# Moving the squares behind the casts at the entry of the first up projection

## The chip, the cores and the metric

One core of a Trainium2 chip runs the whole computation in one launch. The metric is the device time of that launch in microseconds. The engines that matter here are TensorE (PE, matmuls), VectorE (DVE), ScalarE (ACT), GpSimd (POOL), and SyncE (SP), which only issues the loads.

## The reference, cut to what matters

The reference is two blocks of two layers each over 512 positions of width 1024. The change touches the first layer's pool mixer and the entry of the first conv FFN:

```python
x = x + pool_mixer(rmsnorm(x, norm_mix[0]), pool_w[0], pool_scale[0])
x = x + conv_ffn(rmsnorm(x, norm_ffn[0]), ffn_up[0], ffn_conv[0], ffn_conv_b[0], ffn_down[0])
...
def conv_ffn(h, w_up, conv_w, conv_b, w_down):
    u = h @ w_up                                  # 1024 -> 2 * 2816
    up = jnp.pad(u, ((0, 0), (CONV_W - 1, 0), (0, 0)))
    u = sum(conv_w[j] * up[:, j:j + S] for j in range(CONV_W)) + conv_b
    a, g = u[..., :D_FF], u[..., D_FF:]
    return (jax.nn.silu(g) * a) @ w_down
```

## The kernel before, in words

Activations lie transposed: `x` is eight chunks of 128 rows (features) by 512 columns (positions). Each fp32 matmul operand is split into a rounded high part and the low part that is left, and a product of 128 by 128 by 512 is three matmuls (`three`, L510 to L512): high by high, high by low, low by high. One output bank of the up projection takes eight chunks, so 24 matmuls. This text calls that a product. Products come in pairs: for each `f` of 22, `g = 0` is the a-half and `g = 1` the gate half. The first pair is the first and second product, the next pair the third and fourth. PE runs them in order, `u = f % 2`, into banks `2u` and `2u + 1`.

Weights come in jobs of 1 MB, one job for each pair of products, double-buffered in two slots. SP loads a job into `w_raw` once the low part of the job two before it is done (`load`). ACT copies it to `w_hi` (`split_w`, L1109), once PE has finished the pair that used the slot. DVE subtracts to get `w_lo` (`split_w`, L1684). Job 0 is the pool mixer's, job 1 the first pair's, job 2 the second pair's, job 3 the third pair's. The change calls job 1, 2, 3 the first, second and third split of this stage in that sense.

Each engine has its own instruction queue, written out by hand, and works it off in order. Between the queues stand semaphores. At the entry the work of one chunk `m` of `x` goes like this.

- PE: `mix(m)` of the pool mixer ends.
- DVE: `residual(m)` adds it to `x` (L1701, with a wait for its own write behind it).
- ACT: `hi_of_x` casts `x` times gain to `h_hi` (L1136); DVE: `split_x` makes `h_lo` from `x` and `h_hi` (L1696). PE's first product takes chunk `k` as soon as `h_lo` has it.
- ACT: `square` writes `x` squared to the one buffer `sq` (L1139); POOL: `add` adds it to `sq_sum` (L2517). `square(m)` waits until the add of `m - 1` has freed `sq`.

The normalisation is applied behind the matmul: PE sums `sq_sum` over partitions with a matmul by ones (`stats`, L523), ACT takes the root (`root`), DVE the reciprocal (`norm_factors`, L1690), and then DVE multiplies each finished bank by `rs` into `taps_in` (L1777), which frees the bank. PE meets a full ring at the fifth product, which needs the bank of the first.

ACT's queue has in this order: all casts and squares of the pool stage, then in `conv_up(0)` the second split, `root`, and the loop over `f`. DVE's has: the residuals and low parts, the second split, `norm_factors`, and the loop. In both loops the split for the pair two ahead stands in the body of `f`. `pairs` makes a hardware loop over two `f` at a time and takes the last two (with `peel=1` also the first two) out of it, so that they can differ.

`taps_in` has three columns of zero padding, so it is cleared once; the clearing also gives the four credits of `acc_free` that PE starts with.

Of the kernel before, what the change touches and what calls it, by code (L numbers as in the profile page):

```python
# [27 lines left out]
ALU = mybir.AluOpType  # L28
ACT = mybir.ActivationFunctionType
# [6 lines left out]
ND = D // P  # L36
DFF = 2816
NF = DFF // P
# [157 lines left out]
def build(nc, a, stop_after=None):  # L196
    with ExitStack() as ctx:
# [194 lines left out]
            return (g_hi[:, k], g_lo[:, k]) if n == 2 and k < EARLY else (h_hi[:, k], h_lo[:, k])  # L392

        partner_of = (sq_sum, sq)
        query_of = [qr[c % 3][:] for c in range(ND - 1)] + [taps_in[:, 0, PAD:]]
        y_of = [hid[:, 0], hid[:, 1], sq[:], silu_g[:], taps_in[:, 0, PAD:], taps_in[:, 1, PAD:], hid[:, 0], hid[:, 1]]
        squares_of = (hid[:, 0], hid[:, 1], sq[:], silu_g[:])
# [109 lines left out]
        def _(pe):  # L507
# [43 lines left out]
            def up(n):  # L551
                stage = f"up{n}"

                def body(i):
                    for u in range(2):
                        f, slot = 2 * i + u, (J0[stage] + u) % 2
                        pe.wait_ge(w_lo_done, J0[stage] + f + 1)
                        for g in range(2):
                            pe.wait_ge(acc_free, FREE0[stage] + 2 * f + g - 3)
                            for k in range(ND):  # L560
                                if u == 0 and g == 0:
                                    pe.wait_ge(h_lo_done, H_COUNT[stage] + k + 1)
                                mm = three(bank[2 * u + g][:], *tile_of(slot, g * ND + k), *input_of(n, k),
                                           k == 0, k == ND - 1)
                            mm.then_inc(seg_done, 1)
                            if isinstance(i, int) and 2 * f + g == (1 if n == 0 else 0):
                                (stats_of_both if n == 2 else stats)(stage)
                pairs(pe, NF // 2, body, peel=1)

# [528 lines left out]
        def _(act):  # L1098
            def split_w(j, count=None, segs=None):


                if j >= n_jobs:
                    return
                act.wait_ge(w_loaded[j % 2], 16 * (j // 2 + 1) if count is None else count)
                if j >= 2:

                    act.wait_ge(seg_done, SEGS_BEFORE[j - 1] if segs is None else segs)
                n = TILES[j] * P
                act.activation(w_hi[j % 2][:, 0:n], w_raw[j % 2][:, 0:n], ACT.Copy).then_inc(w_hi_done, 1)  # L1109
# [45 lines left out]
            def conv_up(l):  # L1155
                stage = f"up{l}"
                n0, j0, s0 = l * NF, J0[stage], SEG0[stage]

                split_w(j0 + 1)
                root(stage)  # L1160

                def body(i):
                    for u in range(2):
                        f, j = 2 * i + u, j0 + u + 2

                        if not isinstance(i, int):
                            split_w(j, 16 * (j // 2 + 1) + 16 * i, s0 + 2 * f + 2)
                        elif f < NF - 1:
                            split_w(j0 + f + 2)

                        act.wait_ge(hid_done, n0 + f)
                        for g in (1, 0):
                            wait_apart(acc_free, FREE0[stage] + 2 * f + 2)
                            act.activation(bank[CONV_A + g][:], taps_in[:, g, PAD:], ACT.Identity,  # L1174
                                           bias=col(f"conv{l}_b", g * NF + f), scale=col(f"conv{l}_2", g * NF + f))\
                                .then_inc(seeded, 1)
                        act.wait_ge(tapped, 4 * (n0 + f) + 3)
                        act.activation(silu_g[:], bank[CONV_G][:], ACT.Silu).then_inc(silu_done, 1)
                        wait_apart(hid_done, n0 + f + 1)
                        act.activation(act_hi[:, f], hid[:, u], ACT.Copy).then_inc(act_hi_done, 1)  # L1180
                pairs(act, NF // 2, body)

            def glu_up(n):
                stage = f"up{n}"
# [106 lines left out]
            def pool():  # L1291

                def average_hi(m):
                    act.wait_ge(pool_u_done, m + 1)
                    act.activation(h_hi[:, m], bank[4 + m % 4][:], ACT.Copy, scale=col("mix0", m)).then_inc(pool_hi_done, 1)

                def residual_hi(m):

                    act.wait_ge(seg_done, m // 2 * 2 + 2)
                    act.wait_ge(x_ready, x_before("up0") + m + 1)  # L1300
                    hi_of_x("up0", m)

                act.wait_ge(vec_loaded, 16)
                average_hi(0)
                average_hi(1)
                act.activation(w_hi[0][:, HALF_POOL:], w_raw[0][:, HALF_POOL:], ACT.Copy).then_inc(w_hi_done, 1)
                for m in range(2, 6):
                    average_hi(m)
                split_w(1)
                average_hi(6)  # L1310
                average_hi(7)
                for m in range(ND):
                    residual_hi(m)
                    if m >= 2:
                        act.wait_ge(sq_added, 9 * PREP_OF["up0"] + m - 1)
                        square("up0", m - 2)
                for m in (ND - 2, ND - 1):
                    act.wait_ge(sq_added, 9 * PREP_OF["up0"] + m + 1)
                    square("up0", m)

            def attention_inputs():
                split_w(J0["kproj"] + 1)
# [354 lines left out]
        def _(dve):  # L1677
# [48 lines left out]
            def pool():  # L1726
# [17 lines left out]
                                  ALU.subtract).then_inc(w_lo_done, 1)  # L1744
                average_lo(2)
                average_lo(3)
                dve.memset(taps_in[:], 0.0).then_inc(acc_free, 4)
                for m in range(2):
                    residual(m)
                average_lo(4)  # L1750
                average_lo(5)
                split_w(1)
                for m in (2, 3):
                    residual(m)
                average_lo(6)
                average_lo(7)
                split_x("up0", 0)
# [7 lines left out]
            def conv_up(l):  # L1765
                stage = f"up{l}"
                n0, j0, s0 = l * NF, J0[stage], SEG0[stage]

                split_w(j0 + 1)
                norm_factors(stage)  # L1770

                def body(i):
                    for u in range(2):
                        f = 2 * i + u
                        for g in range(2):
                            dve.wait_ge(seg_done, s0 + 2 * f + g + 1)
                            dve.tensor_tensor(taps_in[:, g, PAD:], bank[2 * u + g][:], rs[:], ALU.mult).then_inc(acc_free, 1)  # L1777
                        if not isinstance(i, int) or f < NF - 1:
                            split_w(j0 + u + 2 if not isinstance(i, int) else j0 + f + 2, j0 + f + 3)
                        for n, (tap, g) in enumerate(((1, 1), (1, 0), (0, 1), (0, 0))):  # L1780
                            if tap == 1:
# [9 lines left out]
                        dve.wait_ge(act_lo_done, n0 + f)  # L1791
                        dve.tensor_tensor(hid[:, u], bank[CONV_A][:], silu_g[:], ALU.mult).then_inc(hid_done, 1)
                        dve.wait_ge(hid_done, n0 + f + 1)
                pairs(dve, NF // 2, body)

            def glu_up(n):
                stage = f"up{n}"
# [708 lines left out]
        def _(pool):  # L2506
# [5 lines left out]

            def add(prep, m):
                n = PREP_OF[prep]
                pool.wait_ge(sq_done, ND * n + m + 1)
                pool.wait_ge(sq_added, 9 * n + m + 1)
                pool.tensor_tensor(sq_sum[:], sq_sum[:], sq[:], ALU.add).then_inc(sq_added, 1)  # L2517

            def squares(prep):
                clear(prep)  # L2520
# [154 lines left out]
                        .then_inc(y_lo, 1)  # L2675

            pool.memset(pool_tap[:], 0.0).then_inc(act_lo_done, 1)
            for stage in enabled:
                if stage.startswith("up"):
                    split_hidden(int(stage[2:]))  # L2680
# [192 lines left out]
```

## Time and profile before

| what | value |
|---|---|
| time, median of 3 runs | 3060.1 us (3057.92 to 3061.3) |
| time of the profiled execution | 3060.17 us |
| its span, first to last instruction | 3058.4 us |
| PE busy | 2989.5 us, 98% of the span |
| DVE, ACT, POOL busy | 1594.9, 1194.0, 528.3 us |
| mean granted TensorE clock | 0.991 |

The profiled execution's time is 1.8 us more than its span, and 0.07 us above the median. The span begins with the first instruction of any engine; all times in the rows below count from there. A busy PE is not PE at its peak, since matmuls are pipelined: a 512-column matmul lasts 0.39 us in the rows but the next starts 0.23 us behind it.

### The profile page before, as it was taken

Reading aid. Unit: us, or ns where it says so; the run is one execution under the profiler, and the core shown is the slowest. Engines: PE = TensorE matmul, PEld = TensorE weight load, DVE = VectorE, ACT = ScalarE, POOL = GpSimd, SP = SyncE. Lnnn points to the kernel's source line nnn. Section 1 sums busy time; section 2 is a strip of 40 time slices with the busy share of each in tenths; the row PEclk is TensorE's granted clock in tenths of the full one; section 3 lists DMA queues with packets and bytes.
Section 4 is the critical chain, followed back from the end, with each engine's and each line's share of the span. In section 5 each row is a group of like instructions: output and inputs, shape, how many; then the busy total and the mean of one; then the engine's idle time right before and its main releaser. Section 6 shows DMA issues by size and latency. Waiting matters only on the chain.

```text
span 3058.4 us, 37147 instructions
## 1 busy us (share of the span) xinstructions
PE 2989.5 (98%) x13546; PEld 2455.6 (80%) x13546; DVE 1594.9 (52%) x1838; ACT 1194.0 (39%) x1589; POOL 528.3 (17%) x516
## 2 busy tenths in 40 slices
PE   7999999999999999999999899999999999999998
PEld 6888877777888888788887688888888887788887
DVE  6665366687566535533338843333433337743332
ACT  5554243488455424322232442222322226532221
POOL 1111011255211112111110211111111104511110
PEclk9999999999999999999999999999999999999999
DMA  4222333200222223222232022222322232222222
GB/s 165 96 96 84 101 119 102 76 1 1 86 97 98 83 94 113 96 96 92 85 112 85 15 83 96 96 89 95 106 96 96 82 110 97 83 97 96 92 86 84
DMA packets 47931, 273.42 MB, mean 89 GB/s; under 512 B 6448, under 2 KB 8160, under 8 KB 25568
## 3 DMA queue, kind: packets, MB, share of 16 engines
q1 hardware_dynamic: 47840, 272.19, 25.7%
q8 instruction: 58, 0.95, 0.1%
q14 instruction: 33, 0.27, 0.0%
HBM read 269.28 MB, written 2.11 MB: 89 GB/s over the span
## 4 chain that ended last, share of the span: by engine, by line
PE 89%; DVE 6%; ACT 2%; issue 1%; POOL 1%; DMA 0%; DVEq 0%; ACTq 0%; SPq 0%; POOLq 0%
PE bank L510 28%; PE bank L512 28%; PE bank L511 28%; PE bank L822 1%; DVE w_lo L1684 1%; ACT probs L1394 1%; PE bank L960 1%; PE bank L728 0%; PE bank L806 0%; DVE rc L2395 0%; PE bank L839 0%; PE bank L838 0%; PE bank L926 0%; PE bank L807 0%; POOL r_lo L2674 0%
## 5 line engine op out<-in xcount | busy, mean ns | idle before, releaser
L510 PE MATMUL bank<-h_hi,w_hi 128*128 128x512 f32 x2448 | 961.7, 393 | 12.9 <-DVE w_lo L1684 7.8
L511 PE MATMUL bank<-h_lo,w_hi 128*128 128x512 f32 x2448 | 955.6, 390 | 0.0
L512 PE MATMUL bank<-h_hi,w_lo 128*128 128x512 f32 x2448 | 955.5, 390 | 0.0
L1684 DVE TENSOR_TENSOR w_lo<-w_raw,w_hi 128x2048 fp32r<-128x2048 f32 (+2 forms) x282 | 575.3, 2041 | 527.8 <-ACT w_hi L1109 527.1
L1109 ACT ACTIVATE w_hi<-w_raw 128x2048 fp32r<-128x2048 f32 (+2 forms) x282 | 474.9, 1684 | 328.3 <-PE bank L512 301.1
L510 PEld LDWEIGHTS bank<-h_hi,w_hi 128*128 128x128 f32 x2448 | 460.3, 188 | 117.0 <-DVE w_lo L1684 11.3
L512 PEld LDWEIGHTS bank<-h_hi,w_lo 128*128 128x128 f32 x2448 | 460.5, 188 | 97.3
L511 PEld LDWEIGHTS bank<-h_lo,w_hi 128*128 128x128 f32 x2448 | 460.5, 188 | 96.4 <-issue 1.9
L510 PE MATMUL bank<-act_hi,w_hi 128*128 128x512 f32 x1056 | 411.6, 390 | 4.4 <-DVE w_lo L1684 4.4
L511 PE MATMUL bank<-act_lo,w_hi 128*128 128x512 f32 x1056 | 411.3, 390 | 0.0
L512 PE MATMUL bank<-act_hi,w_lo 128*128 128x512 f32 x1056 | 411.3, 389 | 0.0
L2542 POOL TENSOR_TENSOR act_lo<-hid,act_hi 128x512 f32 (+1 forms) x132 | 171.8, 1301 | 1274.5 <-ACT act_hi L1202 847.3
L2517 POOL TENSOR_TENSOR sq_sum<-sq_sum,sq 128x512 f32<-128x512 f32 x87 | 123.5, 1420 | 824.3 <-ACT sq L1139 824.3
L510 PEld LDWEIGHTS bank<-act_hi,w_hi 128*128 128x128 f32 x1056 | 198.3, 188 | 46.3 <-DVE w_lo L1684 5.6
L1813 DVE TENSOR_TENSOR hid<-bank,rs 128x512 f32<-128x512 f32 x88 | 60.9, 692 | 331.6 <-PE bank L512 331.6
L512 PEld LDWEIGHTS bank<-act_hi,w_lo 128*128 128x128 f32 x1056 | 198.3, 188 | 41.3
L511 PEld LDWEIGHTS bank<-act_lo,w_hi 128*128 128x128 f32 x1056 | 198.3, 188 | 41.1
L1202 ACT ACTIVATE act_hi<-hid 128x512 f32 (+1 forms) x88 | 55.8, 634 | 410.8 <-DVE hid L1816 410.8
L1136 ACT ACTIVATE h_hi<-x,vec 128x512 fp32r<-128x512 f32 (+1 forms) x72 | 51.9, 723 | 366.2 <-DVE x L1701 366.2
L1701 DVE SCALAR_TENSOR_TENSOR x<-bank,x 128x512 f32 (+1 forms) x72 | 49.7, 691 | 254.1 <-PE bank L512 254.1
L1200 ACT ACTIVATE silu_g<-taps_in 128x512 f32<-128x512 f32 x88 | 55.7, 633 | 264.3 <-DVE taps_in L1810 264.3
L1786 DVE SCALAR_TENSOR_TENSOR bank<-taps_in,vec,bank 128x512 f32<-128x512 f32 x176 | 120.0, 750 | 1.8 <-ACT bank L1174 1.8
(373 smaller groups left out, 3207.3 us busy)
## 6 DMA issues: line engine op xcount, KB each, us to landing
w_raw<-in_w_up SPq DMA_DIRECT2D x132, 1024.0 KB, 4.9
w_raw<-in_w_down SPq DMA_DIRECT2D x96, 704.0 KB, 4.0
w_raw<-in_w_wout SPq DMA_DIRECT2D x12, 1024.0 KB, 4.9
w_raw<-in_w_ple SPq DMA_DIRECT2D x16, 640.0 KB, 3.9
w_raw<-in_w_ein SPq DMA_DIRECT2D x6, 1024.0 KB, 4.9
w_raw<-in_w_kproj SPq DMA_DIRECT2D x4, 1024.0 KB, 5.1
w_raw<-in_w_qproj SPq DMA_DIRECT2D x4, 1024.0 KB, 4.9
w_raw<-in_w_ogate SPq DMA_DIRECT2D x4, 1024.0 KB, 4.9
```

Source lines behind the costliest of these rows:

```text
L510: pe.matmul(out, wh, mh, start=first, stop=False)
L511: pe.matmul(out, wh, ml, start=False, stop=False)
L512: return pe.matmul(out, wl, mh, start=False, stop=final)
L1109: act.activation(w_hi[j % 2][:, 0:n], w_raw[j % 2][:, 0:n], ACT.Copy).then_inc(w_hi_done, 1)
L1136: act.activation(h_hi[:, m], x[:, m], ACT.Copy, scale=col(GAIN[prep], m)).then_inc(h_hi_done, 1)
L1200: act.activation(silu_g[:], taps_in[:, u, PAD:], ACT.Silu).then_inc(silu_done, 1)
L1202: act.activation(act_hi[:, f], hid[:, u], ACT.Copy).then_inc(act_hi_done, 1)
L1684: dve.tensor_tensor(w_lo[j % 2][:, 0:n], w_raw[j % 2][:, 0:n], w_hi[j % 2][:, 0:n].bitcast(F32), ALU.subtract).then_inc(w_lo_done, 1)
L1786: dve.scalar_tensor_tensor(out=acc, in0=taps_in[:, g, PAD - back:PAD - back + T], scalar=col(f"conv{l}_{tap}", g * NF + f), in1=acc, op0=A ...
L1813: dve.tensor_tensor(hid[:, u], bank[2 * u + 1][:], rs[:], ALU.mult).then_inc(acc_free, 1)
L2517: pool.tensor_tensor(sq_sum[:], sq_sum[:], sq[:], ALU.add).then_inc(sq_added, 1)
L2542: pool.tensor_tensor(act_lo[:, f], hid[:, u], act_hi[:, f].bitcast(F32), ALU.subtract)\
```

## The change

The square buffers become two, `sq` and `silu_g`. ACT's queue holds all eight casts first and all eight squares behind them; a square waits only for the add two before it. POOL starts its adds when all eight low parts are done. PE's `stats` moves from behind the second product to behind the third. ACT and DVE issue the third split right behind the second and ahead of `root` and `norm_factors`, and for that the first two `f` are taken out of their loops. DVE's third residual moves ahead of the first split, and the clearing of `taps_in` moves from DVE to the head of POOL's queue. Only the first up projection (`l == 0`, `n == 0`) is meant; other stages keep their order.

```diff
+        first_squares = (sq[:], silu_g[:])
...
-                            if isinstance(i, int) and 2 * f + g == (1 if n == 0 else 0):
+                            if isinstance(i, int) and i == 0 and 2 * f + g == {0: 2}.get(n, 0):
                                 (stats_of_both if n == 2 else stats)(stage)
...
                 split_w(j0 + 1)
+                if l == 0:
+                    split_w(j0 + 2)
                 root(stage)
...
-                        if not isinstance(i, int):
+                        if l == 0 and isinstance(f, int) and f == 0:
+                            pass
+                        elif not isinstance(i, int):
                             split_w(j, 16 * (j // 2 + 1) + 16 * i, s0 + 2 * f + 2)
                         elif f < NF - 1:
                             split_w(j0 + f + 2)
...
-                pairs(act, NF // 2, body)
+                pairs(act, NF // 2, body, peel=1 - l)
...
                 for m in range(ND):
                     residual_hi(m)
+                for m in range(ND):
                     if m >= 2:
-                        act.wait_ge(sq_added, 9 * PREP_OF["up0"] + m - 1)
-                        square("up0", m - 2)
-                for m in (ND - 2, ND - 1):
-                    act.wait_ge(sq_added, 9 * PREP_OF["up0"] + m + 1)
-                    square("up0", m)
+                        act.wait_ge(sq_added, 9 * PREP_OF["up0"] + m)
+                    act.activation(first_squares[m % 2], x[:, m], ACT.Square).then_inc(sq_done, 1)
...
-                dve.memset(taps_in[:], 0.0).then_inc(acc_free, 4)
                 for m in range(2):
                     residual(m)
                 average_lo(4)
                 average_lo(5)
+                residual(2)
                 split_w(1)
-                for m in (2, 3):
-                    residual(m)
+                residual(3)
                 average_lo(6)
                 average_lo(7)
...
                 split_w(j0 + 1)
+                if l == 0:
+                    split_w(j0 + 2)
                 norm_factors(stage)
...
-                        if not isinstance(i, int) or f < NF - 1:
+                        if not isinstance(i, int) or f < NF - 1 and (l or f):
                             split_w(j0 + u + 2 if not isinstance(i, int) else j0 + f + 2, j0 + f + 3)
...
-                pairs(dve, NF // 2, body)
+                pairs(dve, NF // 2, body, peel=1 - l)
...
             def add(prep, m):
                 n = PREP_OF[prep]
+                if n == 0:
+                    pool.wait_ge(h_lo_done, ND)
                 pool.wait_ge(sq_done, ND * n + m + 1)
                 pool.wait_ge(sq_added, 9 * n + m + 1)
-                pool.tensor_tensor(sq_sum[:], sq_sum[:], sq[:], ALU.add).then_inc(sq_added, 1)
+                square = sq[:] if n else first_squares[m % 2]
+                pool.tensor_tensor(sq_sum[:], sq_sum[:], square, ALU.add).then_inc(sq_added, 1)
...
             pool.memset(pool_tap[:], 0.0).then_inc(act_lo_done, 1)
+            pool.memset(taps_in[:], 0.0).then_inc(acc_free, 4)
```

## Rows read from the trace of the kernel before

**Rows 1.** The page: span, and engines of the chain that ended last.

```profile
span 3058.4 us, 37147 instructions
...
PE 89%; DVE 6%; ACT 2%; issue 1%; POOL 1%; DMA 0%; DVEq 0%; ACTq 0%; SPq 0%; POOLq 0%
```

**Rows 2.** Timeline of PE: start, duration, instruction, [idle before, releaser].

```profile
34.17 0.50 PE L510 MATMUL bank<-h_hi,w_hi 128*128 128x512 f32 x1 [0.59 <-DVE x L1701]
...
37.55 0.50 PE L510 MATMUL bank<-h_hi,w_hi 128*128 128x512 f32 x1 [1.04 <-DVE h_lo L1696]
...
41.58 0.79 PE L510 MATMUL bank<-h_hi,w_hi 128*128 128x512 f32 x1 [1.03 <-DVE h_lo L1696]
...
45.23 0.39 PE L510 MATMUL bank<-h_hi,w_hi 128*128 128x512 f32 x1
...
50.71 1.02 PE L523 MATMUL bank<-sq_sum,ones 128*128 128x512 f32 x2
...
51.80 0.40 PE L511 MATMUL bank<-h_lo,w_hi 128*128 128x512 f32 x1
...
62.47 0.39 PE L510 MATMUL bank<-h_hi,w_hi 128*128 128x512 f32 x1
...
2584.06 0.58 PE L510 MATMUL bank<-h_hi,w_hi 128*128 128x512 f32 x1 [3.86 <-DVE w_lo L1684]
```

**Rows 3.** Windows: stretch, length, busy of five engines (instructions), clock, DMA, GB/s.

```profile
42.00:43.00 1.00, 1.00 (x3) 0.74 (x3) 1.00 (x2) 0.00 (x0) 1.00 (x1) 0.50 0.00 0
...
2586.00:2587.00 1.00, 1.00 (x4) 0.71 (x4) 1.00 (x1) 0.99 (x3) 0.76 (x2) 0.50 1.01 418
```

**Rows 4.** Timeline of DVE around the entry.

```profile
20.35 0.92 DVE L1747 MEMSET taps_in<- 128x1030 f32 x1 [0.16 <-issue]
...
28.11 1.53 DVE L1701 SCALAR_TENSOR_TENSOR x<-bank,vec,x 128x512 f32<-128x512 f32 x2
29.68 1.41 DVE L1730 SCALAR_TENSOR_TENSOR h_lo<-bank,vec,h_hi 128x512 fp32r<-128x512 f32 x2
...
35.39 0.74 DVE L1701 SCALAR_TENSOR_TENSOR x<-bank,vec,x 128x512 f32<-128x512 f32 x1
36.17 1.33 DVE L1696 SCALAR_TENSOR_TENSOR h_lo<-x,vec,h_hi 128x512 fp32r<-128x512 f32 x1
...
40.21 3.67 DVE L1696 SCALAR_TENSOR_TENSOR h_lo<-x,vec,h_hi 128x512 fp32r<-128x512 f32 x3
47.85 2.29 DVE L1684 TENSOR_TENSOR w_lo<-w_raw,w_hi 128x2048 fp32r<-128x2048 f32 x1 [3.98 <-ACT w_hi L1109]
...
56.08 1.29 DVE L1777 TENSOR_TENSOR taps_in<-bank,rs 128x512 f32<-128x512 f32 x2 [0.24 <-DVE rs L1690]
```

**Rows 5.** Source views of L1696 and L1684: durations in ns, minimum, median, maximum.

```profile
L1696 DVE SCALAR_TENSOR_TENSOR h_lo<-x,vec,h_hi x72: 737/752/1782, 31.0 to 2686.4; 128x512 fp32r<-128x512 f32 x42, - x30
...
L1684 DVE TENSOR_TENSOR w_lo<-w_raw,w_hi x282: 557/2291/3354, 25.9 to 3032.6; 128x2048 fp32r<-128x2048 f32 x84, 128x1408 fp32r<-128x1408 f32 x48, 128x1280 fp32r<-128x1280 f32 x8, 128x384 fp32r<-128x384 f32 x1
```

**Rows 6.** Timeline of POOL, at the entry and at two later places.

```profile
31.20 1.70 POOL L2517 TENSOR_TENSOR sq_sum<-sq_sum,sq 128x512 f32<-128x512 f32 x1 [29.90 <-ACT sq L1139]
...
44.06 1.28 POOL L2517 TENSOR_TENSOR sq_sum<-sq_sum,sq 128x512 f32<-128x512 f32 x1 [0.74 <-ACT sq L1139]
...
609.04 1.26 POOL L2578 TENSOR_TENSOR oq<-qr,oq 64x512 fp32r<-64x512 f32 x1 [0.17 <-POOL oq L2578]
...
1194.07 1.32 POOL L2532 TENSOR_TENSOR sq_sum<-sq_sum,sq 128x512 f32<-128x512 f32 x1 [1.91 <-ACT sq L1224]
1195.36 1.74 POOL L2535 TENSOR_TENSOR hid<-hid,silu_g 128x512 f32<-128x512 f32 x1
```

**Rows 7.** Timeline of ACT around the entry.

```profile
43.36 0.63 ACT L1139 ACTIVATE sq<-x 128x512 f32<-128x512 f32 x1 [1.72 <-POOL sq_sum L2517]
45.38 0.63 ACT L1139 ACTIVATE sq<-x 128x512 f32<-128x512 f32 x1 [1.39 <-POOL sq_sum L2517]
45.91 1.91 ACT L1109 ACTIVATE w_hi<-w_raw 128x2048 fp32r<-128x2048 f32 x1
```

## The prediction

> **What bounds the kernel now.** I read the page first. The chain that ended last lies on PE for 89% of the span of 3058.4 us [rows 1], and the profiled execution took 3060.17 us, 0.07 above the median of the runs, so the sum below can be added to that median. What delays PE at the entry is carried to the end unless something behind it waits on another engine. Second comes PE's timeline from the first to the fifth product. PE should do a matmul each 0.227 us (47 of them lie between 51.80 and 62.47) [rows 2]. The first product starts at 34.17 and the second only at 45.23, 11.06 us later, where 24 matmuls need 5.45. The reader sees two causes: three waits of about 1.04 us for low parts (two stand in the rows), and a slow stretch behind the last of them. From 41.58 to 45.23 lie 9 matmuls that would take 2.04 us and took 3.65, so it cost 1.6, and the granted clock there is 0.50, the 1.2 GHz level [rows 2, 3]. Third comes DVE: the three waits follow its rhythm of residual and low part. A low part takes 1.33 us there and 1.22 in the group of three [rows 4], but over all 72 of its kind the minimum is 0.737 and the median 0.752 [rows 5]. The slow ones lie where POOL adds squares (44.06, among others, beside the group of three that runs to 43.88) [rows 4, 6]. Fourth come ACT and POOL: the last square starts at 45.38, 0.04 us behind the end of an add (44.06 + 1.28), and the cast of the second split only 0.53 behind that, at 45.91 [rows 6, 7]. Its low part runs from 47.85 to 50.14 [rows 4]. PE reaches the statistics at 50.71 and needs the second split right after [rows 2]. So before, two chains end almost together: low parts and first two products at 50.71, second split at 50.14.
>
> **The DVE chain.** With the adds held back, a low part costs its median 0.75, or 0.67 from start to start (two of nearly the same kind take 1.41 together) [rows 4, 5]. A residual costs 0.78 to the next start, with its wait (35.39 to 36.17) [rows 4]. The first split ends where it did, since it waits for its cast, and one of the two residuals at 28.11 now stands ahead of it. So the first low part starts at 28.11 + 0.78 + 2 x 0.67 = 30.23. Behind it stand 8 low parts and 4 residuals: 8 x 0.67 + 4 x 0.78 + 0.08 = 8.56, and the last ends at 38.79 instead of 40.21 + 3.67 = 43.88, 5.1 us earlier. The casts, 0.7 apart or more, keep ahead.
>
> **The first two products.** PE is through with the mixer at 33.58 (34.17 less the 0.59 idle before it) [rows 2], and by then its first bank and the first chunks are ready: the residual that frees the bank comes at 31.57. Chunk 5 waits for a low part that ends at 37.45, chunk 7 for the one at 38.79, so its three matmuls run to 39.57, and the second product to 39.57 + 5.48 (45.23 to 50.71) = 45.05. That is a gain of 5.66 us: the waits and the slow stretch are gone.
>
> **What is late next.** The second split. Its cast stands in ACT's queue behind all eight squares, and the eighth square waits for the sixth add. The adds now begin only at 38.79 + 0.07 = 38.86 (a square that ended at 43.99 released an add at 44.06) [rows 6, 7]. Each add also waits for the one before. The adds of before show no such back-to-back pair, since the square lay between. The nearest is the pair of POOL operations at 609.04 with 0.17 idle between them for their own semaphore; adds that follow each other without that wait start 1.29 apart [rows 6]. I take 1.28 + 0.17 = 1.45, the case with the wait, and keep 1.29 as the lower end. The upper end is 1.70, the one add at the entry that met two low parts of DVE [rows 6]. Step by step: sixth add ends at 38.86 + 5 x 1.45 + 1.28 = 47.39; square starts at 47.43; cast at 47.96, ends at 49.87; low part of the weights from 49.90, 2.29 us [rows 4, 7]. The eighth add runs until 50.29 beside it; for that I add 0.2. The second split is ready at about 52.4. A full overlap could make the low part 3.35, the maximum of its line [rows 5]: 1.1 more at the upper end.
>
> The price by rule instead of row: in the Trainium skill, GPSIMD Engine Reference, section Instruction dispatch, a two-input body needs about 2.5 cycles an element, which at that page's 1.2 GHz is an estimate of 1.07 us for 512. Six adds would then end about 1.3 us sooner, and the forecast would be about 2 us above before instead of 3.3. The adds here lasted 1.28 at best [rows 6], so the sum goes by the row.
>
> **The pause and the clock.** PE has nothing from 45.05 to 52.4: the statistics, which filled 50.71 to 51.5, are behind the third product now, and the third product is what waits. Queued behind it is all of PE. A pause of 3.86 us elsewhere left the clock at 0.50 still two to three us after the restart [rows 2, 3]. The slow stretch at the entry cost 1.6, and I charge that again; below it nothing (the clock keeps its 2.4 GHz level), above it a whole third product at the half rate, 5.45.
>
> **The statistics and the fifth product.** Third product 52.4 + 1.6 + 5.45 = 59.45, then statistics. All adds end by 50.29, so they don't wait. Before, from the statistics to the fifth product there were two products, 50.71 to 62.47 or 11.76; now there is one, 6.31. That gives 65.76 for the fifth product against 62.47: **3.3 us later**. The root, the reciprocal and the first `taps_in` keep their lag: 56.08 + 0.69 - 50.71 = 6.06 behind the statistics, so the first bank is free at 65.5, just in time (0.25 to spare, and that margin doesn't move with the pause). The third split comes right behind the second, done by about 54.7, ahead of its need at 65.8. The fourth split now follows the first `taps_in` and taps; DVE reaches it some 9 to 10 us behind the first `taps_in`, at about 75.5, and PE needs it at 65.76 + 10.9 = 76.6. That is the thinnest cover behind the entry, about 1 us; without it that much is paid.
>
> **Edits costed at nothing.** Clearing `taps_in` cost DVE 0.92, but there DVE next waits for the mixer's products and casts; on POOL it lies in 29.90 us of idleness before the first add [rows 4, 6]. The third split early, and the peeled loops, only move work of ACT and DVE under running products; the third split was in time before too, so having it earlier gains nothing. The first two squares run under the last low parts. SP's loads are released by the weights' low parts: job 4's by the second split, 2 us later than before, and it is used more than 15 us behind.
>
> **The sum.** -5.66 (second product's end), +7.35 (pause to 52.4), +1.6 (clock), and the statistics moved, not removed: 65.76 - 62.47 = +3.3 us. 3060.1 + 3.3 = **3063.4 us**. About 0.2%, 6.1 us, is what a measurement of this kernel can tell from no change.
>
> **Rivals.**
>
> - The wait does not appear. If the second split were ready by 45.05 as before it was ready ahead of PE, the whole 5.66 would stay: 3054.4. For it: the waits and the slow stretch that vanish are real. Against it: the cast stands behind the eighth square, and even at 1.29 for an add it can't be ready before 51.4. The sign turns where the second split is ready by about 49. Chance 0.04, and even then the gain is just below 0.2%.
> - The low parts don't get faster without the adds, because they are slow for another reason (both operands new, a pointer scalar). Then each takes 1.24 from start to start, the last ends 8 x 0.57 = 4.6 us later, and with it adds, second split and all behind: +7.9, 3068. Against it: the median of 0.752 in all other places [rows 5]. It decides, as slower by over 0.2%, from about 1.02 a low part on. Chance 0.05.
> - The slow clock lasts through the third product: 5.45 instead of 1.6, so +7.1, 3067.2. For it: the pause is twice any that I found before a product. Against it: 2.4 GHz came back within some 3.5 us in the stretches read. Chance 0.05.
> - Adds at 1.70 and a low part of 3.35: five starts at 0.25 more and a sixth duration of 0.42 more, and 1.1 less the 0.2 charged: +2.6 more, 3066. Inside the range.
>
> **How the numbers follow.** The likeliest, a pause of about 7 us with a price of 1.5 to 6, has 0.86. Its low end is 1.29 an add (-0.8) and no slow stretch (-1.6): 3061.0; its high end is 3066. The runs of before spread from 2.2 below to 1.2 above their median, so I take 3059.5 to 3067. Slower by over 0.2% holds the two rivals at 3067 to 3068 and the top of the likeliest case, 0.11; faster by over 0.2% is left 0.02 for what I don't see; within 0.2% has 0.87.
>
> **What would show it.** Right: low parts (L1696) of 0.75 at the entry, the last ending near 38.8; no half-rate matmuls in the first product; eight adds in a row from 38.9, about 1.45 apart; PE idle before the third product, released by `w_lo`, for about 7 us; half-rate matmuls behind it; the fifth product near 65.8. Wrong: low parts of over 1 us, an add pitch far from 1.45, a second split ready before 49, or a fifth product that waits for its bank or a seventh for the fourth split.

## The result, and the profile after

The changed kernel takes 3065.14 us (median of 20 runs, 3062.57 to 3065.89) against 3059.94 for the kernel before (20 runs, 3057.66 to 3061.6). That is 5.2 us more, a ratio of 1.0018 with an interval from 1.0012 to 1.0024. The forecast was 3063.4 in a range from 3059.5 to 3067. Two executions of well over 4000 us, one of `e7_third_late` (4603.08) and one of the kernel before in the same session (5987.33), are left out of the medians below.

The profiled execution has a span of 3062.0 us (its time is 3063.8). Its entry began 1.17 us earlier than in the profile before: the low part of the first split starts at 24.73 instead of 25.90 [rows 4]. So each time of before has 1.17 taken off when it is compared with this trace. First the page:

```profile
span 3062.0 us, 37083 instructions
...
PE 89%; DVE 7%; ACT 2%; issue 1%; POOL 1%; DMA 0%; DVEq 0%; ACTq 0%; SPq 0%; POOLq 0%
```

Its shares hardly differ from [rows 1]; 5 us in 3060 are not to be found there. The chain of the stretch from 34 to 70 us tells it (start, duration, what ended last):

```profile
35.50 2.09 DVE h_lo L1699 x3
37.66 1.30 POOL sq_sum L2524
39.12 1.30 POOL sq_sum L2524
...
44.95 1.27 POOL sq_sum L2524
46.35 0.43 issue
46.78 1.90 ACT w_hi L1110
48.71 2.54 DVE w_lo L1687
51.29 0.79 PE bank L511
```

Read it from the top. The last low part releases the first add, six adds follow one another, the sixth lets ACT do the eighth square and the cast of the second split, DVE makes its low part, and only then does PE's third product begin. PE's timeline:

```profile
36.31 0.50 PE L511 MATMUL bank<-h_hi,w_hi 128*128 128x512 f32 x1 [0.49 <-DVE h_lo L1699]
...
43.73 0.39 PE L513 MATMUL bank<-h_hi,w_lo 128*128 128x512 f32 x1
51.29 0.79 PE L511 MATMUL bank<-h_hi,w_hi 128*128 128x512 f32 x1 [7.17 <-DVE w_lo L1687]
...
56.15 0.63 PE L513 MATMUL bank<-h_hi,w_lo 128*128 128x512 f32 x1
...
59.52 1.02 PE L524 MATMUL bank<-sq_sum,ones 128*128 128x512 f32 x2
...
65.84 0.39 PE L511 MATMUL bank<-h_hi,w_hi 128*128 128x512 f32 x1
```

The three waits of [rows 2] are down to one of 0.49, and the second product ends at 43.96 (43.73 and one step of 0.23), where before it ended at 50.71 - 1.17 = 49.54. Then comes a wait of 7.17 us for the second split. The third product takes 59.52 - 51.29 = 8.23 us instead of 5.45, because 12 of its matmuls, and most of a thirteenth, run at the half rate. The windows show it (columns as in [rows 3], the granted clock third from the right):

```profile
50.00:51.00 1.00, 0.00 (x0) 0.00 (x0) 1.00 (x1) 0.47 (x1) 0.00 (x0) 0.50 0.00 0
52.00:53.00 1.00, 1.00 (x4) 0.81 (x3) 1.00 (x1) 0.00 (x0) 0.00 (x0) 0.50 0.51 115
56.00:57.00 1.00, 1.00 (x4) 0.72 (x4) 0.00 (x0) 0.00 (x0) 0.00 (x0) 0.52 0.98 393
57.00:58.00 1.00, 1.00 (x6) 0.82 (x5) 0.00 (x0) 0.00 (x0) 0.00 (x0) 1.00 0.83 336
```

It had fallen to the 1.2 GHz level in the pause (0.50 while PE does nothing), and came back to 2.4 GHz only at 57.0, 5.7 us after the restart. The fifth product starts at 65.84; the same point was 62.47 - 1.17 = 61.30 before. So the entry costs 4.5 us in the profiled executions. The medians of the whole kernel differ by 5.2. The two profiled times differ by 3.6 only (3063.8 against 3060.17), because the changed kernel's began its entry 1.17 us earlier; from the first split to the end of the span the two traces differ by 4.8.

DVE, POOL and ACT at the entry, in this order, and the source view of the eight low parts (ns, minimum, median, maximum):

```profile
24.73 2.29 DVE L1687 TENSOR_TENSOR w_lo<-w_raw,w_hi 128x2048 fp32r<-128x2048 f32 x1 [0.39 <-ACT w_hi L1110]
...
35.50 2.08 DVE L1699 SCALAR_TENSOR_TENSOR h_lo<-x,vec,h_hi 128x512 fp32r<-128x512 f32 x3
48.71 4.73 DVE L1687 TENSOR_TENSOR w_lo<-w_raw,w_hi 128x2048 fp32r<-128x2048 f32 x2 [11.13 <-ACT w_hi L1110]
```

```profile
0.78 0.96 POOL L2685 MEMSET taps_in<- 128x1030 f32 x1
...
37.66 1.29 POOL L2524 TENSOR_TENSOR sq_sum<-sq_sum,sq 128x512 f32<-128x512 f32 x1 [35.47 <-DVE h_lo L1699]
39.12 1.29 POOL L2524 TENSOR_TENSOR sq_sum<-sq_sum,silu_g 128x512 f32<-128x512 f32 x1 [0.17 <-POOL sq_sum L2524]
```

```profile
36.71 0.62 ACT L1322 ACTIVATE silu_g<-x 128x512 f32<-128x512 f32 x1
38.99 0.63 ACT L1322 ACTIVATE sq<-x 128x512 f32<-128x512 f32 x1 [1.66 <-POOL sq_sum L2524]
...
46.24 0.63 ACT L1322 ACTIVATE silu_g<-x 128x512 f32<-128x512 f32 x1 [0.80 <-POOL sq_sum L2524]
46.78 3.69 ACT L1110 ACTIVATE w_hi<-w_raw 128x2048 fp32r<-128x2048 f32 x2
```

```profile
L1699 DVE SCALAR_TENSOR_TENSOR h_lo<-x,vec,h_hi x8: 743/748/752, 29.1 to 36.8; 128x512 fp32r<-128x512 f32 x8
```

All eight low parts lie between 0.743 and 0.752 us. From 37.3 to 46.2 ACT does no more than one square behind each add and waits for the next, with the cast that PE needs behind all of them in its queue.

### The profile page after: what moved, and what is told of

Same layout as the page of the kernel before. It is cut to its first block, busy times and chain, and to the rows that moved or that the text cites. A ratio compares the mean times of both kernels' runs of the same rounds, so it can differ in the third digit from the quotient of the medians.

```text
span 3062.0 us, 37083 instructions
## 1 busy us (share of the span) xinstructions
PE 2987.0 (98%) x13546; PEld 2451.4 (80%) x13546; DVE 1590.0 (52%) x1837; ACT 1170.0 (38%) x1570; POOL 529.2 (17%) x517
## 4 chain that ended last, share of the span: by engine, by line
PE 89%; DVE 7%; ACT 2%; issue 1%; POOL 1%; DMA 0%; DVEq 0%; ACTq 0%; SPq 0%; POOLq 0%
PE bank L511 28%; PE bank L512 28%; PE bank L513 28%; DVE w_lo L1687 1%; PE bank L823 1%; ACT probs L1397 1%; PE bank L949 0%; PE bank L729 0%; DVE cy L2221 0%; PE bank L807 0%; DVE rc L2399 0%; PE bank L839 0%; PE bank L840 0%; PE bank L808 0%; POOL r_lo L2681 0%
```

## The experiments

Each kernel is the changed kernel with one edit, unless told otherwise. Two measures stand beside each other: the median against the median of the kernel before in the same session (3059.4 for the first four, 3058.92 for the next four, one run of 3058.66 for the last two), and from the profiles the lag of the fifth product's first matmul behind the start of the first split's low part. The second leaves out when the first loads land. The expectations are times beside the 3059.94 and 3065.14 of the result; in a session whose kernel before stands lower, the difference against before is the fairer of the two to hold them to. It is 62.47 - 25.90 = 36.57 us before and 65.84 - 24.73 = 41.11 after.

| kernel | median us (runs) | against before | ratio, interval | lag us, against before |
|---|---|---|---|---|
| changed kernel | 3065.14 (20) | +5.2 | 1.0018, 1.0012 to 1.0024 | 41.11, +4.5 |
| e1_cast_third | 3055.33 (11) | -4.1 | 0.9985, 0.9976 to 0.9994 | 32.85, -3.7 |
| e2_busy_pause | 3061.7 (11) | +2.3 | 1.0009, 1.0000 to 1.0018 | 38.56, +2.0 |
| e3_stats_second | 3060.74 (11) | +1.3 | 1.0006, 0.9996 to 1.0015 | 38.68, +2.1 |
| e4_old_squares | 3061.24 (11) | +1.8 | 1.0006, 0.9997 to 1.0015 | 36.10, -0.5 |
| e5_no_hold | 3063.19 (11) | +4.3 | 1.0010, 1.0001 to 1.0019 | 40.64, +4.1 |
| e6_last_by_matmul | 3055.15 (11) | -3.8 | 0.9985, 0.9976 to 0.9994 | 32.27, -4.3 |
| e7_third_late | 3066.28 (10) | +7.4 | 1.0020, 1.0011 to 1.0030 | 44.09, +7.5 |
| e8_dve_as_before | 3065.52 (11) | +6.6 | 1.0019, 1.0010 to 1.0029 | 41.46, +4.9 |
| e9_old_squares_2 | 3056.18 (1) | -2.5 | | 36.12, -0.5 |
| e10_old_squares_3 | 3059.97 (1) | +1.3 | | 37.73, +1.2 |

**Is it the cast behind the eighth square?** `e1_cast_third` moves that one cast up.

```diff
-                split_w(j0 + 1)
+                if l:
+                    split_w(j0 + 1)
...
                     act.activation(first_squares[m % 2], x[:, m], ACT.Square).then_inc(sq_done, 1)
+                    if m == 1:
+                        split_w(J0["up0"] + 1)
```

> The changed kernel with one edit: ACT's cast of the second split stands behind the second square instead of the eighth. Theory (the pause is the second split's cast standing behind the eighth square, and so behind six adds of 1.45 us): the cast then runs at about 37.3 to 39.2 us, its low part on DVE beside the adds, at most 3.4 us, so it is ready by about 42.6, ahead of the end of the second product at 43.96. PE goes straight on, the third product ends at 49.4, the adds at 49.1 or a little later, no half-rate stretch. Fifth product near 55.5 instead of 65.8 in the changed kernel's frame; time about 5 us under before, 3054.5 to 3056. Rival (the later start of the adds itself, or the statistics behind the third product, is what costs): the statistics wait for the adds several us, and the time stays within 2 us of 3065.

It took 3055.33, 4.1 us under the kernel before and some 9 under the changed one. ACT, DVE, POOL and PE of its trace:

```profile
37.49 1.91 ACT L1110 ACTIVATE w_hi<-w_raw 128x2048 fp32r<-128x2048 f32 x1
```

```profile
39.43 3.40 DVE L1690 TENSOR_TENSOR w_lo<-w_raw,w_hi 128x2048 fp32r<-128x2048 f32 x1 [1.59 <-ACT w_hi L1110]
```

```profile
39.38 1.29 POOL L2527 TENSOR_TENSOR sq_sum<-sq_sum,silu_g 128x512 f32<-128x512 f32 x1 [0.17 <-POOL sq_sum L2527]
40.84 3.13 POOL L2527 TENSOR_TENSOR sq_sum<-sq_sum,sq 128x512 f32<-128x512 f32 x1 [0.17 <-POOL sq_sum L2527]
```

```profile
51.41 1.10 PE L524 MATMUL bank<-sq_sum,ones 128*128 128x512 f32 x2 [1.58 <-POOL sq_sum L2527]
...
57.84 0.39 PE L511 MATMUL bank<-h_hi,w_hi 128*128 128x512 f32 x1
```

The second split is ready at 42.83, PE never waits for it, and no matmul of the first five products runs at the half rate. What is left is a wait of 1.58 before the statistics: the low part of the split and the adds now meet. The low part starts within the add of 39.38 and takes 3.40 instead of 2.29; the next add starts within the low part and takes 3.13 instead of 1.29. So the adds end 2 us later than reckoned. With the later start of this execution taken off (first split at 24.99 here, at 24.73 in the changed kernel), the fifth product came at 57.58, 2.1 us later than the 55.5 that was expected; the time stayed inside 3054.5 to 3056. The rival is out: with adds as late as these, the gain comes all the same.

**What did the half rate cost?** `e2_busy_pause` keeps PE busy in the pause with matmuls whose result nobody reads.

```diff
                             mm.then_inc(seg_done, 1)
+                            if n == 0 and isinstance(i, int) and i == 0 and 2 * f + g == 1:
+                                for _ in range(29):
+                                    pe.matmul(bank[MISC][:], h_hi[:, 0, 0:P], h_hi[:, 0], start=True, stop=True)
```

> The changed kernel with 29 matmuls of 128x128x512 more behind the second product, into a bank that nothing reads, so that PE is busy in the pause; they add work whose result is not used. Theory (the third product took 8.23 instead of 5.45 us only because the clock had fallen in the pause): the extra matmuls last 6.6 us and end before the second split is ready at 51.3; the third product then takes 5.45 us and all behind it comes 2.8 us sooner: about 3062.3. Rival (the half-rate stretch comes from something else at the restart, or costs nothing behind): 3065 as the changed kernel.

```profile
43.74 6.73 PE L569 MATMUL bank<-h_hi 128*128 128x512 f32 x29
51.19 0.50 PE L511 MATMUL bank<-h_hi,w_hi 128*128 128x512 f32 x1 [0.71 <-DVE w_lo L1690]
...
56.77 1.02 PE L524 MATMUL bank<-sq_sum,ones 128*128 128x512 f32 x2
```

The third product now takes 56.77 - 51.19 = 5.58 us instead of 8.23, with the wait for the split where it was. The lag falls by 2.55 and the median stands 2.9 us lower against before. So the half-rate stretch is a term of its own, 2.6 to 2.8 us, on top of the pause.

**Were the statistics to blame?** `e3_stats_second` puts them back.

```diff
-                            if isinstance(i, int) and i == 0 and 2 * f + g == {0: 2}.get(n, 0):
+                            if isinstance(i, int) and i == 0 and 2 * f + g == {0: 1}.get(n, 0):
```

> The changed kernel with the statistics back behind the second product. Theory (the second split decides, not the statistics): the statistics wait for the last add at about 49.1 us and run inside the pause, the third product starts at 51.3 as in the changed kernel, and the 0.86 us that the statistics take behind the third product is saved: about 3064.3, 0 to 1 us under the changed kernel. Rival (moving the statistics is what made the kernel slower): 3060 or less. Second rival (moving them saved several us, because otherwise PE waits for the adds and then for the split): 3067 or more.

```profile
50.28 2.05 PE L524 MATMUL bank<-sq_sum,ones 128*128 128x512 f32 x2 [5.10 <-POOL sq_sum L2524]
52.34 0.80 PE L511 MATMUL bank<-h_hi,w_hi 128*128 128x512 f32 x1
...
54.64 0.46 PE L513 MATMUL bank<-h_hi,w_lo 128*128 128x512 f32 x1
```

This expectation missed. The lag fell by 2.4 us, not by at most 1, and the median by 3.9 against before; 3060.74 lies between the theory's 3064.3 and the rival's 3060 or less, and nearer to the rival. The trace says why. The third product still begins when the second split is there (52.34 lies 26.55 behind the first split's low part, 51.29 in the changed kernel 26.56), so the theory's place is right. But the statistics, at half rate, run inside the pause from 50.28, and the clock is back at 54.64 with 5 slow matmuls instead of 12. The third and fourth product take 64.47 - 52.34 = 12.13 us; in the changed kernel they take 65.84 - 51.29 - 0.86 = 13.69 without the statistics between them. That is 1.56 us less, beside the 0.86 of the statistics. Behind this pause, moving the statistics to the third product was a loss of about 2.4 us in the traces. The other 1.5 of the medians is not located: the traced execution, 3062.04, is 1.3 above the median of its kernel.

**Are the other edits worth anything?** `e4_old_squares` undoes only the squares.

```diff
                 for m in range(ND):
                     residual_hi(m)
-                for m in range(ND):
                     if m >= 2:
-                        act.wait_ge(sq_added, 9 * PREP_OF["up0"] + m)
-                    act.activation(first_squares[m % 2], x[:, m], ACT.Square).then_inc(sq_done, 1)
+                        act.wait_ge(sq_added, 9 * PREP_OF["up0"] + m - 1)
+                        square("up0", m - 2)
+                for m in (ND - 2, ND - 1):
+                    act.wait_ge(sq_added, 9 * PREP_OF["up0"] + m + 1)
+                    square("up0", m)
...
-                if n == 0:
-                    pool.wait_ge(h_lo_done, ND)
...
-                square = sq[:] if n else first_squares[m % 2]
+                square = sq[:]
```

> The changed kernel with the squares and adds in the order and with the one buffer of before; DVE's order, the clearing on POOL, the statistics behind the third product and the early third split stay. Theory (the other edits are worth next to nothing, and only the held-back squares move the time): low parts take 1.2 to 1.3 us again, the three waits of about 1 us and a half-rate stretch in the first product come back, the low parts start 0.78 us sooner than in before, and the time is 0 to 1 us under before, about 3059.3. Rival (another edit, such as the peeled loops or the early third split, carries the loss): 3063 or more.

> The kernel of e4_old_squares once more, for its trace: its times spread from 3055.65 to 3062.9, and the profiled one was at the low end. Theory (the spread is how long PE stays at the half rate behind its short waits for low parts): an execution at 3061 to 3063 shows 8 or more half-rate matmuls more than the one at 3056.84, which showed about 5 at the entry. Rival (the spread comes from when the first loads land): the same number of half-rate matmuls, and the low parts start 3 us or more later.

> The same kernel again, with the same expectations as e9_old_squares_2.

Of the first of the three traces, the source view of the eight low parts, one of them, and PE's waits:

```profile
L1701 DVE SCALAR_TENSOR_TENSOR h_lo<-x,vec,h_hi x8: 741/1162/1587, 28.6 to 38.5; 128x512 fp32r<-128x512 f32 x8
```

```profile
34.39 1.32 DVE L1701 SCALAR_TENSOR_TENSOR h_lo<-x,vec,h_hi 128x512 fp32r<-128x512 f32 x1
```

```profile
37.80 0.50 PE L511 MATMUL bank<-h_hi,w_hi 128*128 128x512 f32 x1 [1.06 <-DVE h_lo L1701]
...
48.43 0.50 PE L511 MATMUL bank<-h_hi,w_hi 128*128 128x512 f32 x1 [0.99 <-DVE w_lo L1689]
...
54.02 1.02 PE L524 MATMUL bank<-sq_sum,ones 128*128 128x512 f32 x2
```

With the adds among the low parts, five of the eight start while an add runs and take 1.00 to 1.59 us; the other three keep 0.74 to 0.75. PE waits 1.06 for two of them. In the trace the fifth product stands 0.5 us ahead of before, as expected. The median does not show it: 1.8 over before, between the theory's 3059.3 and the rival's 3063, with runs from 3055.65 to 3062.9. Of the two repeats one was at 3056.18 and one at 3059.97. The slower one has its third product from 49.11 to 56.30, 7.19 us instead of 5.59, since there the clock fell behind the wait for the second split and not before it; that is 1.6 of the 3.8 us between the two. The theory's eight more half-rate matmuls are not there: both traces have seven at the entry, and a part of another. They lie ahead of that wait in the faster one, where they cost nothing, and behind it in the slower one. (Neither execution came at 3061 to 3063, for which the theory was made.) Another 0.6 is the start (first split at 24.89, not 24.26). The other 1.6 comes far behind the entry: from 1726 to 1728 us the slower one's granted clock is 0.50, and the faster one goes through the same matmuls, from 1722 to 1726, at 1.00. So the other edits by themselves are worth a half microsecond in two of three traces, and nothing that the medians can tell from no change. The traces do not put the loss of the changed kernel with them; the median alone would not exclude a part of it, since its interval reaches 1.0015.

**The hold on POOL.** `e5_no_hold` takes out only the wait of the adds for all low parts.

```diff
-                if n == 0:
-                    pool.wait_ge(h_lo_done, ND)
```

> The changed kernel without POOL's wait for all eight low parts; the squares themselves still wait on ACT behind all casts. Theory (ACT's order alone holds the adds back, the first two squares are ready at 36.8 and 37.3 us against 37.58 for the last low part): the first add starts some 0.8 us sooner, the last one or two low parts take about 1.2 instead of 0.75, and the time moves by less than 1 us, 3064 to 3065.5. Rival (the hold on POOL is what makes the chain late): 3062 or less.

```profile
34.86 2.08 DVE L1699 SCALAR_TENSOR_TENSOR h_lo<-x,vec,h_hi 128x512 fp32r<-128x512 f32 x3
```

```profile
36.24 1.84 POOL L2522 TENSOR_TENSOR sq_sum<-sq_sum,sq 128x512 f32<-128x512 f32 x1 [34.05 <-ACT sq L1322]
38.23 1.29 POOL L2522 TENSOR_TENSOR sq_sum<-sq_sum,silu_g 128x512 f32<-128x512 f32 x1
```

The first add starts about 0.8 us sooner against the first split and lasts 1.84, since it starts within the last low part (36.19 to 36.94). That one was expected to take 1.2 and keeps its 0.75: the one that starts second pays. The third product starts at 50.26, 0.4 sooner in lag than in the changed kernel (26.17 against 26.56), the half-rate stretch is as long, and the median is 3063.19, a little under what was expected and above the rival's 3062. Against before it is +4.3, 0.9 less than the changed kernel's +5.2, so it moved by less than 1 as expected. ACT's order alone holds the adds back; POOL's own wait adds less than a microsecond.

**A shorter chain of adds.** `e6_last_by_matmul` builds on `e1_cast_third` and lets PE take the eighth square itself.

```diff
                 pe.wait_ge(sq_added, 9 * (n + 1))
+                if n == 0:
+                    pe.matmul(bank[STAT][:], ones[:], sq_sum[:], start=True, stop=False)
+                    pe.wait_ge(sq_done, ND)
+                    pe.matmul(bank[STAT][:], ones[:], first_squares[1], start=False, stop=True).then_inc(stat_done, 1)
+                    return
...
-                for m in range(ND):
+                for m in range(ND if PREP_OF[prep] else ND - 1):
                     add(prep, m)
```

The clearing counts two steps of `sq_added` there, so that the counts of the later stages stay.

> As e1_cast_third (the second cast behind the second square), and the eighth square is not added by POOL but brought into the statistics by a second matmul by ones. Theory (in e1_cast_third PE still waited 1.58 us for the last add): POOL's chain is one add, 1.46 us, shorter and the wait goes; the second matmul costs 0.5 to 0.9. Net 0.5 to 1.1 us under e1_cast_third, about 3054.5. Rival (the extra matmul costs as much as the wait): equal to e1_cast_third within 0.3.

```profile
50.88 1.10 PE L525 MATMUL bank<-sq_sum,ones 128*128 128x512 f32 x2 [0.18 <-POOL sq_sum L2532]
51.81 1.02 PE L527 MATMUL bank<-silu_g,ones 128*128 128x512 f32 x2
```

The wait went from 1.58 to 0.18 and the second matmul took its 0.9. The lag is 0.6 us shorter than that of `e1_cast_third`; the medians, 3.8 and 4.1 us under before, don't tell the two apart, so the gain that was expected shows in the trace alone. Both beat the kernel before and the changed one, and `e1_cast_third` is the simpler of them.

**The third split.** The prediction costed its early place at nothing. `e7_third_late` puts it back into the loop.

```diff
                 split_w(j0 + 1)
-                if l == 0:
-                    split_w(j0 + 2)
                 root(stage)
...
                 split_w(j0 + 1)
-                if l == 0:
-                    split_w(j0 + 2)
                 norm_factors(stage)
...
-                        if not isinstance(i, int) or f < NF - 1 and (l or f):
+                        if not isinstance(i, int) or f < NF - 1:
...
-                pairs(dve, NF // 2, body, peel=1 - l)
+                pairs(dve, NF // 2, body)
```

ACT's loop loses its exception and its peeling in the same way.

> The changed kernel with the third split back in the body of the first f, and the loops not peeled. Theory, corrected (behind the third product's statistics there is only one product before the fifth, so the third split in the body stands behind reciprocal and first taps_in and is late): low part of the third split from about 66 to 68.3 us, PE waits about 2.4 us before the fifth product, and the time is 2 to 5 us over the changed kernel, 3067 to 3070. Rival (the prediction's: the third split is in time either way): 3065.

```profile
66.88 2.28 DVE L1683 TENSOR_TENSOR w_lo<-w_raw,w_hi 128x2048 fp32r<-128x2048 f32 x1
```

```profile
69.41 0.47 PE L511 MATMUL bank<-h_hi,w_hi 128*128 128x512 f32 x1 [2.62 <-DVE w_lo L1683]
```

PE waits 2.62 us at the fifth product, and the median stands 2.2 us further from before than the changed kernel's, at the lower end of the 2 to 5 us expected. Its early place is needed, because the statistics moved.

**DVE's order.** `e8_dve_as_before` undoes the other moves on DVE.

```diff
+                dve.memset(taps_in[:], 0.0).then_inc(acc_free, 4)
                 for m in range(2):
                     residual(m)
                 average_lo(4)
                 average_lo(5)
-                residual(2)
                 split_w(1)
-                residual(3)
+                for m in (2, 3):
+                    residual(m)
...
-            pool.memset(taps_in[:], 0.0).then_inc(acc_free, 4)
```

> The changed kernel with DVE's order of before (both residuals behind the first split) and the clearing of taps_in on DVE again. Theory (only the one residual of 0.78 us stands in the chain, the clearing lies in a wait): first low part, adds, second split and all behind come 0.8 us later, 3065.9. Rival (the chain starts at ACT's casts and DVE's order is worth nothing): 3065.1. Second rival (the clearing on DVE counts too): 3066.8.

```profile
25.09 2.29 DVE L1687 TENSOR_TENSOR w_lo<-w_raw,w_hi 128x2048 fp32r<-128x2048 f32 x1 [1.05 <-ACT w_hi L1110]
...
30.19 1.41 DVE L1699 SCALAR_TENSOR_TENSOR h_lo<-x,vec,h_hi 128x512 fp32r<-128x512 f32 x2
...
49.85 4.74 DVE L1687 TENSOR_TENSOR w_lo<-w_raw,w_hi 128x2048 fp32r<-128x2048 f32 x2 [11.13 <-ACT w_hi L1110]
```

The first low part comes 5.10 us behind the start of the first split (25.09) where it was 4.32 in the changed kernel, so the one residual is worth its 0.78, and the second split's low part is late by the same (24.76 against 23.98). The clearing on DVE adds nothing to that: behind it DVE still waits 1.05 us for the cast of the first split. At the fifth product only 0.35 is left, since this execution had 10 half-rate matmuls and not 12. The medians don't decide between the three: 3065.52 lies between the theory and the first rival, but against before it is +6.6, 1.4 over the changed kernel's +5.2, between the theory's 0.8 and the second rival's 1.7. It is the trace that speaks for the theory.

## Why the prediction was right, step by step

**What bounds the entry.** Right. The waits for low parts, but for one of 0.49, and the slow stretch of before are gone in the trace after, and PE's chain takes the rest.

**The DVE chain.** Right: 0.75 a low part (0.743 to 0.752), and the last ends at 37.58, where 38.79 - 1.17 = 37.62 was forecast. That the adds slow the low parts, which the prediction took from the two kinds of rows, is borne out by the three traces with the adds among them (1.00 to 1.60 us for those that start beside an add) against all traces with the adds behind them (0.75). Its rival, low parts that stay slow for a reason of their own, fell.

**The second product.** Right: 43.96 against 45.05 - 1.17 = 43.88.

**What is late next.** Right in place and size. The adds start 1.43 to 1.47 apart with 0.17 idle between them, the sixth ends at 46.21 (46.22 forecast), and the third product starts at 51.29 (51.23). The estimate from the Trainium skill, GPSIMD Engine Reference, section Instruction dispatch, which calls about 2.5 cycles an element a floor, was 1.07 us an add; the adds took 1.26 to 1.30, above that floor, and it was the row that held. The rival without a wait would have needed the second split by 43.96, and it came 7.3 us behind that.

**The pause and the clock.** The mechanism was right, the size was not. The price of the slow stretch was carried over from a pause of another length: 1.6 us, from the 9 matmuls behind three short waits. It was 8.23 - 5.45 = 2.8, and the busy pause of `e2_busy_pause` gave 2.6 of it back. So the term that was mis-sized is the +1.6 for the clock, which measured 2.8. These 1.2 us are all that the forecast lacks in the trace: 3.3 forecast, 4.5 measured at the fifth product. The rival with a whole third product at the half rate was closer here than its chance said, though 12 of 24 were slow and not 24.

**The statistics and the fifth product.** Right in the arithmetic: 65.84 - 59.52 = 6.32 from the statistics, 6.31 forecast, and the bank was free in time. The prediction put the move of the statistics at nothing ("moved, not removed") and didn't ask what they would do inside the pause: left there, they cost nothing and also take up part of the half-rate stretch, 2.4 us together (`e3_stats_second`).

**Edits costed at nothing.** One of them wrongly. "The third split was in time before too, so having it earlier gains nothing" held for the order of before, with two products between the statistics and the fifth. With one product between them the split in the loop stands behind the reciprocal and the first banks, and PE waits 2.6 us for it (`e7_third_late`). The forecast is not touched by that, since the changed kernel has it early. The clearing on POOL and the residual on DVE were costed as they came out. The fourth split was in time: PE has no idle time in the sixth to eighth product of the changed kernel.

**The sum.** 3.3 us forecast, 4.5 in the trace, 5.2 in the medians. The 0.7 between the last two is less than the runs of either kernel spread (over 3 us), and no run shows where it lies. That the profiled execution, 3063.8, stands so near the forecast of 3063.4 is luck: its entry began 1.17 us early, which hides the 1.2 by which the clock term was too small, and its kernel's median is 1.3 higher.

## What to carry to other kernels

A hand-written order has two ends: ask not only what the moved work waits for, but what stands behind it in the same queue, and follow that to the engine that sets the time. Here 5.6 us were won at the front, and 7.2 of waiting and 2.8 of half rate were lost to one cast that stood behind eight squares; moving that cast up kept 3.7 of the 5.6 in the trace. Each pause of 7 us in these traces cost its own length and, unless PE was kept busy in it, a stretch at the half rate behind it; size that stretch by a pause of like length, and let work that has to be done anyway fall into the pause.

## What the runs showed of the hardware

POOL's adds and DVE's instructions with both inputs in SBUF hold each other up, and in the meetings of these traces the one that starts second pays while the first keeps its time. A low part of 128x512 took 0.75 us alone. When it started within an add it took 1.00 to 1.60 (`e4_old_squares` and its repeats; up to 1.78 in the kernel before [rows 5]): one from 34.39 to 35.71 met an add from 33.89 to 35.17, which lasted its usual 1.28. An add that started within a low part took 1.61 to 1.84 instead of 1.29 (`e4_old_squares`, `e5_no_hold`), and that low part kept its 0.75. The low part of a 128x2048 split took 2.29 alone and 3.40 when it started within an add; the add that started within it took 3.13. A residual, which reads one input from a PSUM bank, started at 29.87 within the add from 29.45 to 31.11 of `e4_old_squares` and took its 0.75.

The half-rate stretch behind a pause was not of one length. From the restart to the first matmul at the full rate it lasted 3.4 and 3.8 us in the kernel before, behind waits of 1 and 4 us; behind 7 us of nothing it lasted 4.8 to 6.1 in four traces (10 to 13 matmuls at the half rate, and one in which the rate rose). In the repeats of one and the same kernel it fell into the third product in one execution and ahead of it in the others, which changed the entry by 1.6 us.
